# Mixture of experts on one core: an expert's tokens picked by a matmul with zero-one tiles, biases resident, slot lists made behind expert 0

## The reference, cut to what matters

```python
logits = (h @ w_router + b_router).astype(jnp.float32)
top_val, top_idx = lax.top_k(logits, TOP_K)           # 4 of 32
gates = jax.nn.softmax(top_val, axis=-1)
...
def expert_block(args):
    xe, e = args                                      # the tokens of expert e
    gu = xe @ w_gate_up[e] + b_gate_up[e]             # 1024 -> 2048
    glu, lin = gu[:, :D_FF], gu[:, D_FF:]
    glu = jnp.minimum(glu, SWIGLU_LIMIT)
    lin = jnp.clip(lin, -SWIGLU_LIMIT, SWIGLU_LIMIT)
    act = glu * jax.nn.sigmoid(SWIGLU_ALPHA * glu) * (lin + 1.0)
    return act @ w_down[e] + b_down[e]                # 1024 -> 1024
...
return jax.ops.segment_sum(y_sorted * g_sorted[:, None], sorted_tok, num_segments=T)
```

## Time and profile before

| | |
|---|---|
| median of 3 runs | 1623.16 us (1622.08 to 1630.47) |
| the profiled execution | 1621.99 us |
| its span, first to last instruction | 1620.2 us |
| TensorE matmul busy | 1462.0 us (90%) |
| TensorE weight loads busy | 673.9 us (42%) |
| VectorE / ScalarE / GpSimd busy | 587.1 / 249.2 / 94.7 us |
| mean granted clock of TensorE | 0.975 |
| HBM read | 516.08 MB |
| gate-up matmuls L1018 | 461.8 us for 2048 records, 65.2 us idle before them |
| down matmuls L1035 | 225.1 us for 1024 records |

### The profile page before, as it was taken

The page is one execution under the profiler, slowest core; times in us unless marked ns, Lnnn a source line. Parts: engine busy times, 40 slices in busy tenths (PEclk is TensorE's granted clock), DMA queues, the critical chain, the costliest instruction groups (busy, mean ns, idle before and its releaser), DMA issues.

```text
span 1620.2 us, 19909 instructions
## 1 busy us (share of the span) xinstructions
PE 1462.0 (90%) x7387; PEld 673.9 (42%) x7387; DVE 587.1 (36%) x1072; ACT 249.2 (15%) x496; POOL 94.7 (6%) x142
## 2 busy tenths in 40 slices
PE   5999988998888978999999899999989999999995
PEld 2544555676666653333333233333323333333331
DVE  4106536212551352243243243233324323332435
ACT  1102021245760031010010010000001001000001
POOL 0000000011230011000000000000000000000000
PEclk9999998799999999999999999999999999999998
DMA  9545680634895346999999999999999999999991
GB/s 350 189 156 208 224 276 14 208 103 138 308 333 208 128 182 261 422 414 414 421 413 414 418 422 409 421 421 406 421 421 417 410 414 422 405 410 416 403 413 43
DMA packets 79594, 521.67 MB, mean 322 GB/s; under 512 B 9697, under 2 KB 18471, under 8 KB 51744
## 3 DMA queue, kind: packets, MB, share of 16 engines
q1 hardware_dynamic: 71712, 499.06, 76.8%
q0 software_dynamic: 7840, 22.03, 4.1%
HBM read 516.08 MB, written 8.65 MB: 324 GB/s over the span
## 4 chain that ended last, share of the span: by engine, by line
DMA 50%; PE 41%; DVE 5%; SPq 3%; issue 2%; ACT 0%; DVEq 0%
DMA ring<-in_w_gate_up 45%; PE ps L1018 10%; PE ps L897 6%; PE ps L613 5%; PE ps L777 5%; PE ps L638 4%; PE ps L1035 2%; PE ps L550 2%; DMA ring<-in_w_proj_gla 2%; DMA ring<-in_w_ada 1%; DMA ring<-in_cache_k 1%; PE ps L752 1%; SPq L460 1%; PE ps L585 1%; PE ps L641 1%
## 5 line engine op out<-in xcount | busy, mean ns | idle before, releaser
L1018 PE MATMUL ps<-ring,mem 128*64 128x512 f32 x2048 | 461.8, 597 | 65.2 <-DMA ring<-in_w_gate_up 64.0
L1018 PEld LDWEIGHTS ps<-ring,mem 128*64 128x64 f32 x2048 | 140.7, 137 | 380.3 <-issue 250.2
L1035 PE MATMUL ps<-ring,mem 128*64 128x512 f32 x1024 | 225.1, 592 | 0.0
L1804 DVE TENSOR_SCALAR mem<-ps 128x512 f32<-128x512 f32 x32 | 22.2, 693 | 507.1 <-PE ps L1018 507.1
L1283 ACT ACTIVATE mem<-mem 128x512 f32<-128x512 f32 x32 | 20.2, 632 | 839.1 <-DVE mem L1804 839.1
L1035 PEld LDWEIGHTS ps<-ring,mem 128*64 128x64 f32 x1024 | 72.7, 137 | 147.1 <-issue 136.7
L1821 DVE TENSOR_TENSOR mem<-ps,mem 128x1024 f32<-128x1024 f32 (+1 forms) x96 | 117.2, 1221 | 4.7 <-PE ps L1043 1.2
L1823 DVE TENSOR_TENSOR mem<-mem 128x1024 f32<-128x1024 f32 (+1 forms) x96 | 117.5, 1224 | 3.3
L550 PE MATMUL ps<-mem 128*128 128x128 f32 (+2 forms) x608 | 97.9, 296 | 22.8 <-ACT mem L1236 10.9
L550 PEld LDWEIGHTS ps<-mem 128*128 128x128 f32 (+2 forms) x608 | 77.5, 188 | 84.8 <-issue 42.7
L1043 PE MATMUL ps<-mem 64*128 64x512 f32 (+1 forms) x384 | 103.3, 611 | 1.4 <-DVE mem L1821 1.4
(11 more groups left out here) (296 smaller groups left out, 1138.0 us busy)
## 6 DMA issues: line engine op xcount, KB each, us to landing
ring<-in_w_gate_up SPq DMA_DIRECT2D x128, 2048.0 KB, 26.8
ring<-in_w_down SPq DMA_DIRECT2D x64, 2048.0 KB, 24.4
ring<-in_w_in SPq DMA_DIRECT2D x13, 2048.0 KB, 9.1
ring<-in_w_ada SPq DMA_DIRECT2D x12, 2048.0 KB, 11.7
ring<-in_cache_k SPq DMA_DIRECT2D x64, 256.0 KB, 3.2
ring<-in_cache_v POOLq DMA_DIRECT2D x64, 256.0 KB, 5.1
ring<-in_state_gla SPq DMA_DIRECT2D x2, 2048.0 KB, 11.8
out<-ring SPq DMA_DIRECT2D x2, 2048.0 KB, 8.1
```

The costliest lines, as they stand in the source:

```text
L1018: last = mm(out, xeT[par][:, 2 * s + k, :], w[:, k, 512 * q:512 * q + 512], start=False, stop=s == 3 and k == 1)
L1035: last = mm(ps[64 * f:64 * f + 64, 0, :], actT[:, k, s, :], w[:, k, 512 * f:512 * f + 512], start=False, stop=s == 1 and k == 3)
```

## The change

For each expert VectorE makes a zero-one tile `hot` (token x slot) for each of the three token tiles, by comparing the slot number of each token with a ramp (`token_slots`), and copies one column `sel_e` that selects the expert. TensorE multiplies `h2_tok` (as array weights, 128 features at a time with stride 2, up to 128 tokens deep) with `hot` (moving, 64 columns), summed over the three tiles; the result has features on partitions and is copied to `xeT`. The store of h2, the indirect DMAs, `x_in` and the transposes go. The gate-up biases of all experts are loaded once into `b_gu` (two strips of 32 rows), and the bias matmul has 32 rows, with `sel_e` as weights. The down biases are loaded once into `y_out[1]`, and a combine ahead of down 0 adds them, multiplied by the gates `g_all`, to all tokens at once. The token lists and gates by slot, the broadcasts and the transposes of x move from before expert 0 to between gate-up 0 and down 0, in two PSUM banks instead of four. `xeT` is one tile instead of two, and `x_res` has memory of its own. Sums wait for three more combined tiles, hence the shifted counts.

```diff
-        h2_rows = nc.dram_tensor("h2_rows", [T, D], F32, kind="Internal").ap()
...
-        bias = [part(mem, m0, 3072), part(mem, m0 + 3072, 3072)]
-        x_in = [part(mem, m0 + 6144, D), part(mem, m0 + 7168, D)]
-        xeT = [part(mem, m0 + 8192, KD, BT), part(mem, m0 + 8704, KD, BT)]
+        b_gu = part(mem, m0, 1024)
+        x_res = part(mem, m0 + 1024, 3, D)
+        xeT = part(mem, m0 + 8192, 4, 2, BT)
...
+        hot = [part(mem, r0 + 2152, 3, BT), part(mem, r0 + 2344, 3, BT)]
+        g_all = part(mem, m0 + 11776, 3, P)
...
-        x_res = h2_tok
...
-            def expert_bias(e, par):
-                sp.dma_start(bias[par][0:1, 0:2 * D], b_gate_up[0, bass.ds(e, 1), :]).then_inc(b_land[par], 16)
-                sp.dma_start(bias[par][0:1, 2 * D:3 * D], b_down[0, bass.ds(e, 1), :]).then_inc(b_land[par], 16)
...
-            for t, (t0, n) in enumerate(TILES):
-                sp.wait_ge(h2t_sb, 2 * t + 2)
-                sp.dma_start(h2_rows[t0:t0 + n, :], h2_tok[0:n, t, :]).then_inc(h2_out, 16)
+            sp.wait_ge(pj_sb, 24)
+            for half in range(2):
+                sp.dma_start(b_gu[32 * half:32 * half + 32, :], b_gate_up[0, :, 1024 * half:1024 * half + 1024]).then_inc(bias_in, 16)
+            sp.wait_ge(zero_sb, 1)
+            for half in range(2):
+                sp.dma_start(y_out[1][64 * half:64 * half + NE, :], b_down[0, :, 512 * half:512 * half + 512]).then_inc(bias_in, 16)
...
-                    sp.wait_ge(slot_used, e * RING - RING)
-                    expert_bias(e, par)
...
+            def gather(par, n):
+
+                pe.wait_ge(hot_sb, n + 1)
+                for j in range(KD):
+                    c0 = 512 * (j % 2) + 2 * P * (j // 4) + j // 2 % 2
+                    for t, (_, rows) in enumerate(TILES):
+                        last = mm(ps[:, 0, j * BT:(j + 1) * BT], h2_tok[0:rows, t, c0:c0 + 2 * P - 1:2], hot[par][0:rows, t, :],
+                                  start=t == 0, stop=t == 2)
+                last.then_inc(xe_ps, 1)
+
+            def gate_up_bias(par):
+
                 for q in range(4):
...
-            def xe_transposes(par, gathered):
-
-                pe.wait_ge(x_land[par], gathered)
-                pe.sem_inc(turns, 1)
-                for k in range(KD):
-                    c0 = 2 * P * (k // 2) + k % 2
-                    last = tr(ps[:, 0, k * BT:(k + 1) * BT], x_in[par][0:BT, c0:c0 + 2 * P - 1:2], BT)
-                last.then_inc(xe_ps, 1)
-
-            def gate_up_bias(par, biases):
-
-                pe.wait_ge(b_land[par], biases)
-                for q in range(4):
-                    out = ps[64 * (q % 2):64 * (q % 2) + 64, 2 + q // 2, :]
-                    mm(out, const("row0"), bias[par][:, 512 * q:512 * q + 512], start=True, stop=False)
-
-            def gate_up(par, n, weights):
+                    rows = slice(32 * (q // 2), 32 * (q // 2) + 32)
+                    mm(ps[64 * (q % 2):64 * (q % 2) + 64, 2 + q // 2, :], sel_e[rows, par:par + 1].to_broadcast([32, BT]),
+                       b_gu[rows, 512 * (q % 2):512 * (q % 2) + 512], start=True, stop=False)
+
+            def gate_up(n, weights):
                 pe.wait_ge(xe_sb, n + 1)
                 for s in range(PRE):
                     pe.wait_ge(land[s], weights + land0[s])
...
                     for k in range(2):
                         for q in range(4):
                             out = ps[64 * (q % 2):64 * (q % 2) + 64, 2 + q // 2, :]
-                            last = mm(out, xeT[par][:, 2 * s + k, :], w[:, k, 512 * q:512 * q + 512], start=False, stop=s == 3 and k == 1)
+                            last = mm(out, xeT[:, 2 * (s % 2) + k, s // 2, :], w[:, k, 512 * q:512 * q + 512], start=False, stop=s == 3 and k == 1)
...
-                for f in range(2):
-                    mm(ps[64 * f:64 * f + 64, 0, :], const("row0"), bias[par][:, 2048 + 512 * f:2560 + 512 * f], start=True, stop=False)
...
+            def expert(par, n):
 
                 pe.wait_ge(y_sb, n)
-                xe_transposes(1 - par, turn * 16)
+                gather(1 - par, n + 1)
                 pe.wait_ge(spread_sb, n)
                 for t in range(2):
-                    pe.wait_ge(gated_sb, n * 3 + (t - 4))
+                    pe.wait_ge(gated_sb, n * 3 + (t - 1))
                     combine(1 - par, t, 4 + 2 * ((1 - par + t) % 2), comb_ps)
-                down(par, n, (n + 1) * 16, n + 2)
-                pe.wait_ge(gated_sb, n * 3 - 2)
+                down(n, (n + 1) * 16, n + 2)
+                pe.wait_ge(gated_sb, n * 3 + 1)
                 pe.sem_inc(turns, 1)
                 combine(1 - par, 2, 4 + 2 * ((3 - par) % 2), comb_ps)
-                gate_up_bias(1 - par, turn * 32)
-                gate_up(1 - par, n + 1, (n + 2) * 16)
-
-            pe.wait_ge(ix_done, 1)
-            pe.wait_ge(h2t_sb, 16)
-            gate_up_bias(0, 32)
-            pe.wait_ge(hot2_sb, 1)
+                gate_up_bias(1 - par)
+                gate_up(n + 1, (n + 2) * 16)
+
+            pe.wait_ge(bias_in, 64)
+            pe.wait_ge(h2t_sb, 6)
+            gather(0, 0)
+            gate_up_bias(0)
+            gate_up(0, 16)
+
+            gather(1, 1)
+            pe.wait_ge(pair_sb, 1)
             for j in range(3 * TOPK):
                 nn = TILES[j // TOPK][1]
-                last = mm(ps[0:BT, 7, BT:BT + NCOL], row_oh[0:nn, j, :], col_oh[0:nn, j, :], start=j == 0, stop=j == 3 * TOPK - 1)
-            last.then_inc(gsl_ps, 1)
-
-            xe_transposes(0, 16)
-            gate_up(0, 0, 16)
-
-            xe_transposes(1, 16)
-            down(0, 0, 16, 2)
-            gate_up_bias(1, 32)
-            gate_up(1, 1, 32)
-
-            pe.wait_ge(y_sb, 1)
-            xe_transposes(0, 32)
-            pe.wait_ge(spread_sb, 1)
-            combine(0, 0, 4, comb_ps)
-            combine(0, 1, 6, comb_ps)
-            down(1, 1, 32, 3)
+                last = mm(ps[0:BT, 7, 0:2 * NCOL], row_oh[0:nn, j, :], pair_oh[0:nn, :, j, :], start=j == 0, stop=j == 3 * TOPK - 1)
+            last.then_inc(slots_ps, 1)
+            for t, (t0, n) in enumerate(TILES):
+                last = tr(ps[:, 6, t0:t0 + n], g_all[0:n, t, :], n)
+            last.then_inc(gall_ps, 1)
+            pe.wait_ge(gate_x_sb, 1)
+            for i in range(10):
+                if i > 1:
+                    pe.wait_ge(h2t_sb, i + 5)
+                for q in range(4):
+                    m, bank, cols = 4 * (i % 2) + q, 4 + i % 2, slice(q * P, (q + 1) * P)
+                    if i < 2:
+                        last = mm(ps[:, bank, cols], modT[:, 5, m, 0:1].to_broadcast([P, P]), ident, start=True, stop=True)
+                    elif i < 4:
+                        last = mm(ps[0:NS_TOK, bank, cols], gate_x[:, m, :], ident, start=True, stop=True)
+                    else:
+                        t0, n = TILES[(i - 4) // 2]
+                        last = tr(ps[0:n, bank, cols], xT[:, m, t0:t0 + n])
+                last.then_inc(h2t_ps, 1)
+            pe.wait_ge(slots_sb, 1)
+            combine(1, 0, 6, comb_ps)
+            pe.wait_ge(h2t_sb, 16)
+            combine(1, 1, 4, comb_ps)
+            down(0, 16, 2)
             pe.wait_ge(gated_sb, 1)
-            combine(0, 2, 4, comb_ps)
-            gate_up_bias(0, 64)
-            gate_up(0, 2, 48)
+            combine(1, 2, 6, comb_ps)
+            gate_up_bias(1)
+            gate_up(1, 32)
+
+            expert(1, 1)
...
+            tokens_in(0)
+            sigmoid(0)
+            tokens_in(1)
+            act_rows(0)
...
             dve.wait_ge(rank_ps, 1)
+            for t, (t0, n) in enumerate(TILES):
+                v.scalar_tensor_tensor(slot1[0:n, t, 0:NE], ps[0:n, 4, NE * t:NE * t + NE], 1.0, pick[0:n, t, :], ALU.add, ALU.mult)
+            link(v.tensor_copy(sel[:, 0:NE], const("stack")))
+
+            def token_slots(par, n):
+                for t, (_, rows) in enumerate(TILES):
+                    v.tensor_scalar(hot[par][0:rows, t, :], const("iota")[0:rows, :], 1.0, slot1[0:rows, t, bass.ds(n, 1)], ALU.add, ALU.is_equal)
+                v.tensor_copy(sel_e[:, par:par + 1], sel[:, bass.ds(n, 1)]).then_inc(hot_sb, 1)
+
+            token_slots(0, 0)
             v.memset(pos, 0.0)
+            v.memset(slot1[:, :, NE:NCOL], 0.0)
+            v.memset(g_all, 0.0)
...
+                last = v.tensor_tensor(rtmp[0:n, t0:t1].rearrange("p t k e -> p (t k) e"), oh[0:n, t0:t1].rearrange("p t k e -> p (t k) e"),
+                                       g.to_broadcast([n, TOPK * (t1 - t0), NE]), ALU.mult)
+            link(last)
+            for t, (_, n) in enumerate(TILES):
+                last = v.tensor_reduce(g_all[0:n, t, 0:NE], rtmp[0:n, t].rearrange("p k e -> p e k"), AX, ALU.add)
+            link(last)
+            v.tensor_copy(g_all[:, :, 64:64 + NE], g_all[:, :, 0:NE]).then_inc(pair_sb, 1)
...
+            token_slots(1, 1)
             activated(0)
-            dve.wait_ge(gsl_ps, 1)
```

(81 more changed lines are left out.)

188 lines of the change are left out of this document (68 added, 120 removed).

## The result

The changed kernel takes 1855.05 us (median of 4 runs, 1851.59 to 1856.32) against 1626.66 us for the kernel before (4 runs): a ratio of 1.140, 95% interval 1.136 to 1.144. I had forecast 1655 us, in a range of 1630 to 1695. The direction was right and the size was not: 228 us slower instead of 32.

A forecast was written before the change was run, and what follows sets the result against it. The prediction took DMA as the bound before and TensorE after: 28.17 us per expert plus the terms gave 31.8; with the start and 30 periods, 1622.0 + 32.7 = 1655 us, range 1630 to 1695.

The forecast's parts named there:

- What bounds the kernel, and what the change does to it: Expert loop: DMA bounds before, 31.2 us per expert; after the change TensorE does, 31.8 against 30.4.
- the whole sum: TensorE's time per expert: 28.17 us plus and minus the terms of the change gives 31.8 us.
- The half-height third tile (64 rows) gets no discount: Gather matmuls: records on the 64-row token tile priced like those on 128 rows, 0.12 us each.
- 48 x 0.12 = 5.76: New gather on TensorE: 48 records per expert, 0.12 us apart, add 5.76 us.
- The clock: TensorE in the expert loop: records priced at full clock, with no term for a fall.
- Rival (a), strided weights cost double: Gather: a real matmul's stride-2 weight load makes a record cost 0.24 us; about 1839 us in all, chance 0.12.
- My sign for (a): Profile after: a gather of over 8 us per expert would show the forecast wrong and strided weights slow.
- Gate-up bias at 0.88 less: Gate-up bias matmuls: four 32-row by 64-column matmuls run at once on four array corners, -0.88 us per expert.
- case (c): Gate-up bias: the four array corners run only in pairs, no gain, 1681 us; chance 0.18.
- Down bias and the wait for the activation: Between combine and down: activation wait shrinks, -0.2 us; down bias goes but bares a wait for ScalarE, -0.1 us.
- The start: Before the expert periods: gate-up 0 at 610.2 us, 11.3 us earlier; gate-up 1 at about 653.5.
- a gap of 1.3 us: Start: TensorE has no gap above this before gate-up 0, so full clock was assumed, running 610.2 to 624.0.

The follow-up runs named there:

- e6_swap: Changed kernel with gather operands exchanged (one-hot tile as weights, tokens moving, 12 records), down 0 moved earlier, one-hot tiles made two experts ahead: 1609.31 us.
- e1_pad: Changed kernel with the gather's third token tile padded from 64 to 128 rows with zeros: 1676.56 us.
- e4_inter: Changed kernel with the next expert's gather spread in four pieces of 12 records among the gate-up matmuls: 1755.52 us.
- e3_unit: Changed kernel with the gather's weights read at stride 1 instead of 2, so part of the result uses other features: 1842.41 us.
- e7_interpad: Changed kernel with both the third tile padded to 128 rows and the gather spread in pieces among the gate-up matmuls: 1708.46 us.
- e2_outer: Changed kernel with the gather's loops exchanged, token tile outside and feature chunk inside: 1725.52 us.
- e5_outerpad: Changed kernel with the gather's loops exchanged and the third tile padded to 128 rows: 1678.47 us.

## Why the prediction was wrong, point by point

**What bounds the kernel, and what the change does to it: right.** The DMA period without gathers and biases is 30.3 us (e6_swap: 12.58 MB at 415 GB/s, period 30.3), TensorE becomes the bound, and the kernel is slower. With the padded tile the whole sum can be tested: 1676.6 us against 1655, period 32.3 against 31.8.

**"The half-height third tile (64 rows) gets no discount": the step that failed.** I asked whether 64 rows are cheaper and found no. I did not ask what it costs that records of two heights alternate. In the earlier trace rows every spacing that I read, 0.109 and 0.12, came from runs of one height. The 14 changes of 0.14 us that padding takes away are 2.0 us per expert at full clock, 60 us in 30 periods. The term "48 x 0.12 = 5.76" is right for one height (e1_pad: 5.97 with the last record's tail), was 8.0 for two at full clock (8 chunks of 1.00 us), and 9 to 11 us with the clock's fall.

**The clock: a term that the sum did not have.** I took 1.00 for granted because TensorE would be busy all the time. It is, and the clock falls all the same (0.85 in the gather, 0.62 behind it). This is the larger part. Of the 5.6 us between the period of the changed kernel and that of the padded one (37.93 and 32.29), 2.0 are the changes of height; the other 3.6, some 110 us in 30 periods, go to the clock. e4_inter, which only breaks the stretch, agrees: it is 100 us faster although spreading costs it 26 us, and it has three changes of height less per expert, 13 us. The page "TensorE: Matmul & The Clock Gate" of the Trainium skill ("Why this matters for your kernels") puts drops in mid-kernel down to idle gaps of TensorE; by that rule there would be none here, and the trace shows them with TensorE busy 8.90 of 8.90 us.

**Rival (a), strided weights cost double: wrong, though its 1839 us was near the result.** e3_unit takes the stride away and wins 13 us. My sign for (a), a gather of over 8 us, did appear, with another cause. A number that comes out right is no evidence for the mechanism.

**Gate-up bias at 0.88 less: right in the mechanism, 0.75 in size.** L978 takes 1199.33 to 1200.35, 1.02 us for the eight records that took 1.77. The mix of row and column tiles does run side by side; case (c) falls. This agrees with what the Trainium skill ("TensorE: Matmul & The Clock Gate", "Part 3: Packing small matmuls") states, that row and column tiles compose.

**Down bias and the wait for the activation: small, and not quite as I had it.** TensorE still waits for ScalarE's copy ahead of down (0.91 us at 1191.31). The padded period is 0.5 us above my sum in small pieces: gather 5.9, bias 1.0 and gate-up 13.88 are each 0.1 above their term, activation and down together another 0.1.

**The start: right in order, 17 us short.** The one-hot tile comes at 604.8 (I had 603.4), and gate-up 0 starts at 618.9, 2.5 us earlier than before instead of 11.3. I argued that a gap of 1.3 us would not bring the clock down and took the full clock. It was full when the gather began, and fell 1.5 to 2 us into it. That happens in the padded kernel as well, so the half-empty records are not its cause, or not the only one. Ahead of both, TensorE had been idle in part:

```profile
603.00:604.80 1.80, 0.48 (x5) 0.36 (x4) 1.26 (x10) 0.98 (x7) 0.00 (x0) 1.00 1.02 437
604.80:609.00 4.20, 4.20 (x20) 3.62 (x20) 3.83 (x21) 0.00 (x0) 0.00 (x0) 0.68 0.14 59
```

In e1_pad the first gather still takes 9.06 us, where the later ones take 5.97, and its clock is 0.50 from 607 to 614. What brings it down there stays open. Gate-up 1 starts 10 us earlier in e1_pad, at 660.5: its first two gathers are 7.0 us shorter together, the matmuls behind the second 1.2, and the routing happened to end 1.8 us sooner.

## What to carry to other kernels

Price a group of matmuls by its shape and by the shape of its neighbours: a tile of other height or width than the one before cost about 0.14 us each time here, so put equal shapes next to each other, or pad the odd one with zeros. A busy TensorE does not always have its full clock: here a gather of 48 narrow records, a third of them on half of the rows, halved it for its own end and for the combine behind it. So read the granted clock of the stretch. And try the long operand on the moving side: 12 records of 512 columns did what 48 of 64 did in 2.9 us, or 3.5 with the transposes that this needs, against 6.0 for the padded 48 and 9 to 11 for the unpadded.

## What the runs showed of the hardware

- Adding 64 rows of zeros to a matmul made a kernel 178 us faster (1855 to 1677, e1_pad).
- Records on 128 rows and on 64 rows: 0.12 us apart on 128 rows, 0.20 to 0.22 at a change, 0.17 behind it, both ways; 0.14 us per change (e7_interpad against e4_inter too).
- The clock went from 1.00 (2.4 GHz) to half (1.2 GHz) within a gather of narrow, partly half-empty records with TensorE busy throughout. With full rows and the same timing it stayed at 2.4 GHz between experts (e2_outer against e5_outerpad, 47 us). Spread over pieces of 2 us it stayed up as well (e4_inter).
- A change between 64-column strips and full width cost 0.14 us (e7_interpad).
- What remains open: why the clock fell in 21 of 30 periods of e2_outer and not in the other nine, with the same records; what part the narrow moving side has, which no run varied by itself; and why the first gather lost the clock with full rows too.
